# A two-layer transformer kernel: norms by half rows, and the first layer's stages in another order

## The reference, cut to what matters

```python
# layer one (first_block)
xn = rmsnorm(h, ln1_w); proj = xn @ w_in
dq, dk, dv, gq, gk, gv, gr, zf, zb = jnp.split(proj, splits, axis=-1)
log_g_f = jax.nn.log_sigmoid((zf @ gla_gate_w2_f + gla_gate_b_f)) / GLA_TAU      # and _b
da = rmsnorm(diff_attention(dq, dk, dv, lam, pos), da_subln_w) * (1.0 - lam_init)
go = rmsnorm(gla_bidirectional(gq, gk, gv, log_g_f, log_g_b), gla_norm_w) * jax.nn.silu(gr)
h = h + jnp.concatenate([da, go], axis=-1) @ w_out
hn = rmsnorm(h, ln2_w)
h = h + peer_ffn(hn, peer_w_q, peer_sub_keys, peer_u, peer_v)
# layer two (hybrid_layer), after the final norm of layer one
m = g[:, :, 0] * y_a + g[:, :, 1] * y_b + g[:, :, 2] * y_c
h = h + m @ w_o
hn = rms_norm(h, norm2_g)
gate, up = jnp.split(hn @ w_gate_up, 2, axis=-1)
h = h + (jax.nn.silu(gate) * up) @ w_down
out = rms_norm(h, final_g)
```

## Time and profile before

| | us |
|---|---|
| three runs | 2654.69, 2650.17, 2654.87 |
| median | 2654.69 |
| profiled execution, device time | 2648.79 |
| profiled execution, span | 2647.0 |
| TensorE busy | 2582.6 (98%) |
| VectorE busy | 1530.2 (58%) |
| GpSimd busy | 1026.9 (39%) |
| ScalarE busy | 925.0 (35%) |
| mean granted TensorE clock | 0.989 of full |

### The profile page before, as it was taken

One profiled execution on the slowest core, in us unless ns is written; L12 is line 12 of the kernel. 1 busy time (PEld: TensorE's weight loads), 2 busy tenths in 40 slices (PEclk: granted clock), 3 DMA queues, 4 the chain that ended last, 5 costly groups with the idle time before them and its releaser, 6 DMA issues.

```text
span 2647.0 us, 33693 instructions
## 1 busy us (share of the span) xinstructions
PE 2582.6 (98%) x12573; PEld 2118.5 (80%) x12573; DVE 1530.2 (58%) x3293; ACT 925.0 (35%) x1472; POOL 1026.9 (39%) x683
## 2 busy tenths in 40 slices
PE   8999889999999999999999999999999999999998
PEld 7776678888888888888888888877977788788886
DVE  3234736999688522225888888843974445433322
ACT  4223533333344322223333333453334442422222
POOL 4320110389888888604777777210350000000000
PEclk9998999999999999999999999999999999999999
DMA  4210046755657766658999999832332123333321
GB/s 155 72 32 33 33 126 211 241 127 137 148 124 195 195 144 145 147 164 288 376 370 366 373 370 370 308 105 80 86 90 56 41 83 132 87 97 96 96 96 72
DMA packets 330946, 427.87 MB, mean 162 GB/s; under 512 B 58720, under 2 KB 246912, under 8 KB 330272
## 3 DMA queue, kind: packets, MB, share of 16 engines
q1 hardware_dynamic: 271392, 358.39, 41.9%
q0 software_dynamic: 59392, 67.34, 10.4%
HBM read 362.59 MB, written 63.05 MB: 161 GB/s over the span
## 4 chain that ended last, share of the span: by engine, by line
PE 82%; ACT 1%; DVE 1%; issue 1%; DMA 0%; SPq 0%; DVEq 0%; ACTq 0%
PE bank L209 26%; PE bank L213 26%; PE bank L212 26%; PE bank L2500 1%; PE bank L1688 1%; PE bank L2475 1%; PE bank L1671 1%; PE bank L2458 0%; PE bank L2498 0%; ACT s_wh L2219 0%; ACT s_junk L375 0%; PE bank L2488 0%; PE bank L475 0%; PE bank L2510 0%; DVE s_h L2814 0%
## 5 line engine op out<-in xcount | busy, mean ns | idle before, releaser
L1727 DVE TENSOR_TENSOR pe_wl<-pe_raw,pe_wh 128x1024 fp32r<-128x1024 f32 x272 | 354.5, 1305 | 367.1 <-ACT pe_wh L1587 350.6
L1517 POOL DMA_INDIRECT scratch_sums<-pe_pick,pe_cell_u x256 | 430.0, 1680 | 78.0 <-issue 77.5
L209 PE MATMUL bank<-pe_xh,pe_wh 128*128 128x512 f32 x1152 | 453.2, 393 | 1.3 <-DVE pe_xl L452 1.3
L213 PE MATMUL bank<-pe_xh,pe_wl 128*128 128x512 f32 x1152 | 448.6, 389 | 0.0
L212 PE MATMUL bank<-pe_xl,pe_wh 128*128 128x512 f32 x1152 | 448.5, 389 | 0.0
L1587 ACT ACTIVATE pe_wh<-pe_raw 128x1024 fp32r<-128x1024 f32 x272 | 288.0, 1059 | 304.2 <-PE bank L213 272.9
L2562 DVE TENSOR_TENSOR s_wl<-s_raw,s_wh 128x1024 fp32r<-128x1024 f32 x143 | 179.4, 1256 | 273.6 <-ACT s_wh L2219 272.3
L209 PE MATMUL bank<-pe_wh,pe_hh 128*128 128x512 f32 x768 | 298.8, 389 | 0.0
L212 PE MATMUL bank<-pe_wl,pe_hh 128*128 128x512 f32 x768 | 298.8, 389 | 0.0
L213 PE MATMUL bank<-pe_wh,pe_hl 128*128 128x512 f32 x768 | 298.8, 389 | 0.0
L209 PEld LDWEIGHTS bank<-pe_xh,pe_wh 128*128 128x128 f32 x1152 | 216.4, 188 | 46.4 <-issue 1.2
(11 more groups left out here) (452 smaller groups left out, 4652.6 us busy)
## 6 DMA issues: line engine op xcount, KB each, us to landing
pe_raw<-in_peer_u SPq DMA_DIRECT2D x128, 512.0 KB
pe_raw<-in_peer_v SPq DMA_DIRECT2D x128, 512.0 KB
scratch_hidden<-pe_a_out SPq DMA_DIRECT2D x128, 256.0 KB
pe_a_in<-scratch_hidden SPq DMA_DIRECT2D x128, 192.0 KB
s_raw<-in_w_in SPq DMA_DIRECT2D x48, 512.0 KB, 3.8
s_raw<-in_w_gate_up SPq DMA_DIRECT2D x44, 512.0 KB, 4.0
scratch_sums<-pp_zeros SPq DMA_DIRECT2D x16, 1024.0 KB, 6.2
pe_added_gate<-scratch_sums SPq DMA_DIRECT2D x32, 512.0 KB
```

The lines of the kernel that those rows point to most:

```text
L209: first = pe.matmul(out, lhs[0], rhs[0], start=start, stop=False, skip_group_check=skip)
L213: return pe.matmul(out, lhs[1], rhs[0], start=False, stop=stop, skip_group_check=skip)
L1517: pool.indirect_dma_start(cells, bass.IndirectOffsetOnAxis(ap=cell_u[:, t, at:at + 1], axis=0), pick[:, t, 2, at:at + 1], None, compute_op ...
L1727: dve.tensor_tensor(wl[:, i % RING, :], raw[:, i % RAW, :], wh[:, i % RING, :].bitcast(F32), ALU.subtract).then_inc(S["w_lo"], 1)
```

## The change

It has parts in every stage but the experts' stream and the first half of layer two.

1. Gate logits: three banks by turns in place of two; three of them before gk, the fourth and fifth after gk's first and second slab.
2. The lambda is made before q is taken, its exponentials beside those of the decays, its last two steps after the keys are rotated.
3. The mask of the last chunk tile comes after `take(k_b)`.
4. ScalarE squares three of four tiles of linear attention's output in the projection's block, one head at a time, with the sum in the same instruction. Only the last tile is squared and summed in the attention's block, and the root stands before the loop.
5. The transposes of head 0 stand at the end of the projection's list, those of head 1 before the loop, of heads 2 and 3 in turns 0 and 1, each with banks of its own.
6. `phase_mix_out` waits for the turned columns one by one; it squares the rows of h by halves; it loads the first four weight tiles of the experts and splits two of them. `SummedStats` in the next block adds the halves and takes one root for all four tiles.
7. `wo` 0 to 3 has banks 4 to 7 and `wo` 4 to 7 has banks 0 to 3.
8. `HalfStats` for norm two and the last norm: squares of the first half rows during `wo` 5 and `down` 12, with a root on a dummy value behind them; adds of the next tile ahead of the wait for the root; the last norm's gain is multiplied into the first half at `down` 14, and at the end ScalarE scales the first half and VectorE the second.

```diff
+class HalfStats(RowStats):
+    def square(self, act, half, t):
+        done = half * NT + t
+        if done:
+            act.wait_ge(self.squared, done)
+        act.activation(self.junk[:, 0:BANK], self.rows[:, t, half * BANK:(half + 1) * BANK], ACT.Square,
+                       accum_out=self.ss[:, half, t:t + 1]).then_inc(self.squared, 1)
+    def first_squares(self, act, ready):
+        for t in range(NT):
+            ready(act, t)
+            self.square(act, 0, t)
+        act.wait_ge(self.squared, NT)
+        act.activation(self.root[:, NT:NT + 1], self.junk[:, 0:1], ACT.Sqrt)
+    def first_means(self, dve, chain):
+        dve.wait_ge(self.squared, NT)
+        chain(dve.tensor_scalar(self.ss[:, 0, :], self.ss[:, 0, :], 1.0 / self.width, EPS, ALU.mult, ALU.add))
+    def on_scalar(self, act, ready, after=None):
+        for t in range(NT):
+            ready(act, t)
+            self.square(act, 1, t)
+            act.wait_ge(self.meaned, t + 1)
+            act.activation(self.root[:, t:t + 1], self.ss[:, 1, t:t + 1], ACT.Sqrt).then_inc(self.rooted, 1)
+            if after and t:
+                after(t - 1)
+        if after:
+            after(NT - 1)
+    def on_vector(self, dve, chain, use, front):
+        front(0)
+        for t in range(NT):
+            dve.wait_ge(self.squared, NT + t + 1)
+            dve.scalar_tensor_tensor(self.ss[:, 1, t:t + 1], self.ss[:, 1, t:t + 1], 1.0 / self.width,
+                                     self.ss[:, 0, t:t + 1], ALU.mult, ALU.add).then_inc(self.meaned, 1)
+            if t + 1 < NT:
+                front(t + 1)
+            dve.wait_ge(self.rooted, t + 1)
+            chain(dve.reciprocal(self.rstd[:, t:t + 1], self.root[:, t:t + 1]))
+            use(t)
+class SummedStats(RowStats):
+    def on_scalar(self, act, ready):
+        act.wait_ge(self.meaned, 1)
+        act.activation(self.root[:, :], self.ss[:, :], ACT.Sqrt).then_inc(self.rooted, 1)
+    def on_vector(self, dve, chain, use, front=None):
+        chain(dve.tensor_tensor(self.ss[:, :], self.halves[:, 0, :], self.halves[:, 1, :], ALU.add))
+        dve.tensor_scalar(self.ss[:, :], self.ss[:, :], 1.0 / self.width, EPS, ALU.mult, ALU.add)\
+            .then_inc(self.meaned, 1)
+        dve.wait_ge(self.rooted, 1)
+        chain(dve.reciprocal(self.rstd[:, :], self.root[:, :]))
+        for t in range(NT):
+            use(t)
...
 phase_project_1, TensorE
-            for t, n in tiles:
-                if t >= 2:
-                    pe.wait_ge(S["y_taken"], t - 1)
+            def gate_logits(t):
+                n = tiles[t][1]
+                if t >= 3:
+                    pe.wait_ge(S["y_taken"], t - 2)
...
-            gemm.on_tensor(pe, gk_b)
+            for t in range(3):
+                gate_logits(t)
+            def logits_after(i):
+                if i < 2:
+                    gate_logits(3 + i)
+            gemm.on_tensor(pe, gk_b, between=logits_after)
...
+            pe.wait_ge(S["rotated"], 2)
+            pe.wait_ge(gemm.bank_free, gemm.freed(gr_b))
+            for b, src in ((0, L["q"]), (4, L["k"])):
+                for t in range(NT):
+                    pe.transpose(bank[:, b, t * P:(t + 1) * P], src[:, t, 0:P], ident)
 phase_project_1, VectorE
-            for t in range(NT):
+            for t in range(NT - 1):
+                mask_chunk(t)
             take(k_b)
+            chain(mask_chunk(NT - 1))
 phase_diff_attention, ScalarE
+            act.activation(qT[:, 0, :], bank[:, Q_BANK[0], :], ACT.Copy, scale=DA_DIM ** -0.5).then_inc(q_ready, 1)
+            act.activation(sq[:, :, :], mix_g[:, NT - 1, :].rearrange("p (h v) -> p h v", h=GLA_HEADS), ACT.Square)\
+                .then_inc(squared, 1)
+            take_query(1)
+            act.wait_ge(mean, 1)
+            act.activation(root[:, :], ss[:, :], ACT.Sqrt).then_inc(rooted, 1)
...
+                if r + 2 < DA_HEADS:
+                    take_query(r + 2)
 phase_diff_attention, TensorE
+            head_columns(1)
+            pe.wait_ge(q_ready, 2)
+            pe.wait_ge(k_ready, 2)
...
+                if r + 2 < DA_HEADS:
+                    pe.wait_ge(k_ready, 2 + r)
+                    head_columns(r + 2)
 phase_diff_attention, VectorE
+            take_key(0)
+            dve.wait_ge(k_turned, 1)
+            dve.tensor_copy(kT[:, :, 0:META], ...)
+            norm_sums()
+            take_key(1)
 phase_mix_out
             def turned(kt):
-                if kt < HALF_K:
-                    pe.wait_ge(turn.done, kt + 1)
+                pe.wait_ge(turn.done, kt + 1)
...
-                    pe.wait_ge(turn.done, KD)
+            for i in range(RAW):
+                sp.dma_start(raw[:, i, :].rearrange("p (k j) -> p k j", k=KD), query_slab(io, i))\
+                    .then_inc(weights_ahead[i], 16)
+            squares(0)
+            for i in range(SPLIT_AHEAD):
+                act.wait_ge(weights_ahead[i], 16)
+                act.activation(wh[:, i, :], raw[:, i, :], ACT.Copy).then_inc(split, 1)
+            squares(1)
 SecondPlan
-                first = 4 * (half if kind == "wo" else 1 - half)
+                first = 4 * (1 - half)
 phase_second
+                if (kind, n) == ("wo", 5):
+                    norm_2.stats.first_squares(act, ...)
+                if (kind, n) == ("down", KF // 2 + 1):
+                    last_stats.first_squares(act, ...)
+            def scale_first(t):
+                act.wait_ge(S["last_rstd"], t + 1)
+                act.activation(h[:, t, halves[0]], h[:, t, halves[0]], ACT.Copy, scale=last_stats.rstd[:, t:t + 1])\
+                    .then_inc(S["front_done"], 1)
+                if (kind, n) == ("down", KF // 2 + 3):
+                    last_stats.first_means(dve, chain)
+                    dve.wait_ge(S["row_landed"], 16)
+                    for t in range(NT):
+                        last = dve.tensor_tensor(h[:, t, halves[0]], h[:, t, halves[0]], final_row[:, halves[0]], ALU.mult)
+                    chain(last)
+            def scale_last(t):
+                dve.sem_inc(S["last_rstd"], 1)
+                dve.scalar_tensor_tensor(h[:, t, halves[1]], h[:, t, halves[1]], last_stats.rstd[:, t:t + 1],
+                                         final_row[:, halves[1]], ALU.mult, ALU.mult).then_inc(S["out_done"], 1)
```

189 lines of the change are left out of this document (122 added, 67 removed).

## The result

| | before | after |
|---|---|---|
| median of the runs, us | 2652.88 (2650.17 to 2654.87) | 2628.97 (2626.47 to 2629.51) |
| profiled execution, us | 2648.79 | 2628.91 |
| its span, us | 2647.0 | 2626.8 |
| TensorE busy, us | 2582.6 | 2575.2 |

The ratio is 0.9909, with a 95% interval of 0.9892 to 0.9926. The forecast was 22.0 us less than before, 2632.7 us. Between the two profiled executions it is 19.9 us less, between the medians 23.9. The sum is compared with the profiled executions, since its terms were read from one; the kernel before varies by 4.7 us in its four runs, so the median does not test it more closely.

A forecast was written before the change was run, and what follows sets the result against it. TensorE was taken to bound the kernel, busy 2582.6 of 2647.0 us, so only its waits and low-clock stretches counted. Terms at the boundaries summed to 22.0 us, from the median of 2654.7 to 2632.7 us; range 2618 to 2645.

The forecast's parts named there:

- Logits: Gate logits before gk: three banks remove 2.5 us of waits, plus part of the slow products; gain 3.0 us (1.0 to 3.7).
- Mask: Before v's first product: copies of k go ahead of the last chunk mask; gain 2.9 us (2.3 to 2.9).
- banks: Before wo's first product: other banks remove the wait for VectorE's multiplications; gain 1.7 us (1.5 to 1.7).
- norm two: Before layer two's silu products: the fourth add no longer waits behind a scaling and root; gain 2.4 us (1.8 to 2.9).
- end: After the last product: earlier add, half squares and scaling split over two engines; gain 4.0 us (3.0 to 4.8).
- Attention: Projection to attention: earlier first exponential, no stop for the root; gain 4.0 us (1.5 to 4.8), clock counted as 0.
- rival (b): Attention: the clock does not fall, or only briefly; up to 9.5 us more gained, so 2622 us; chance 0.12.
- Columns: Output projection's second turn: waiting for remainders singly removes 1.7 us, plus slow products; gain 2.5 us (1.7 to 3.3).
- Experts' start: Output projection to experts: squares under products, first transpose 1.0 us and first product 1.1 earlier; gain 1.5 us (0.3 to 3).
- Rival (a): Attention's low clock gets longer, or an order there costs what another gives; 2643 us; chance 0.17.
- (c): Clock stays low to the attention's end and through the output projection's products; 12 us slower, 2667 us; chance 0.03.
- (d): Block ends absorb the parts' gains; only banks, mask and end count, 8.6 us, so 2646 us; chance 0.08.

The follow-up runs named there:

- u_early: Kernel after with the gate logits, the column-by-column waits of the output projection and the half rows of norm two undone; 2633.99 us, ratio to before 0.9946.
- fill_end: fill_three plus 7 identity transposes at the attention loop's first turn without scores and 8 behind its last products; 2619.33 us, ratio to before 0.9883.
- fill_all: fill_three plus gv's second slab rounded earlier, 10 identity transposes among the chunk sums, 8 behind the attention's last products; 2624.40 us, ratio to before 0.9894.
- u_mid: Kernel after with the mask order, the turning of heads in the attention's loop, wo's banks and the last norm undone; 2639.05 us, ratio to before 0.9965.
- u_root: Kernel after with the linear heads' root taken inside the attention's loop instead of before it; 2628.16 us, one run.
- u_sums: Kernel after with the experts' norm squaring full rows at the start of its own block; 2628.50 us, one run.
- fill_x: Kernel after with 22 identity transposes in the idle time between the output projection's last product and the experts' first transpose; 2625.66 us, ratio to before 0.9909.
- fill_a: Kernel after with 6, 4, 4 and 4 identity transposes ahead of the scores of attention turns 1, 2, 7 and 9; 2627.09 us, ratio to before 0.9916.
- fill_three: Kernel after with the fillings of fill_s, fill_x and fill_a together; 2624.70 us, ratio to before 0.9898.
- fill_s: Kernel after with 14 multiplications of a tile of ones in the idle time before the first transposes; 2626.36 us, ratio to before 0.991.

## Why the prediction was right, step by step

The mechanism held in seven of eight places: the waits that the edits were to remove went, but for most of the one before the experts, and the span fell by 20.2 of 22.0 us. That the total is nearer than the steps is luck: an over-rated term, the logits, and chance in two stretches that nobody edited (1.95 us together) were made up by the attention and the columns.

- Logits, forecast 3.0 (1.0 to 3.7), measured 0.05: the step that failed. The term of 2.5 us for waits was read from the 6.87 us of the logits by taking all above 0.86 us for each as waiting. At full clock no more than 0.15 us of each is waiting; nearly all the rest is the low clock, which had come at 36.8, during the third logit (windows above). The low stretch is 6.8 us long in both profiles with two banks (before, u_early), 3.4 in eight of those with three, and absent in the other four, the kernel after among them. To gv's first product this is 19.8, 18.5 and 16.9 us, so the edit did win 1.3 to 2.9 us there, by the clock and not by waits. The sentence that the later fifth add "costs nothing" was wrong: I looked at the matmuls 40 us away and not at what stands behind the exponentials in ScalarE's list. That is the split of gv's second slab, and the wait for it costs 1.3 us from gv to the chunk sums (28.9 against 27.6 in u_early). In the kernel after the clock then stayed low longer, from 90.3 to 97.1 (3.4 us in the kernel before), which cost 0.47 and 1.06. In the fourteen profiles the stretch from the first logit to the turn of ks takes 80.9 to 81.2 us in twelve, 79.5 in fill_end, which had no fall at 37 and a short one at 90, and 79.7 in fill_all, which had no fall at 37 and not the new wait.
- Mask 2.96, banks 1.87, norm two 2.49, end 3.74: as forecast, and each comes back when undone, the mask and norm two with 1.5 and 1.0 us of low clock on top.
- Attention, forecast 4.0 and 0 for the clock, measured 6.61. The start behaved as worked out: the first exponential comes 4.62 us after the block's start (4.5 by the sum), and the difference of turn 1 is 4.5 us earlier than before, counted from the state of the meta tokens (4.2 to 4.7 by the lists). By the page "ScalarE: Activation LUTs" (What ACT_TABLE_LOAD costs) of the Trainium skill each switch would have held it 1.4 us longer; again the activation starts 1.30 us after the load does. The other 2.1 us were won in the turns behind it, where the clock counted for nothing in the forecast: it was low for 17 us in place of 34. That is part of rival (b), which had 0.12 (its price of 9.5 us makes 2623.2, not 2622). Of the start, u_mid shows 1.6 us for turning heads 2 and 3 in the loop and u_root 0.7 for the root. Repeats of the same attention differ by 3 us, so the 2.1 can be chance.
- Columns, forecast 2.5, measured 3.36: 1.7 of wait (u_early) and 1.6 of clock, which the kernel before lost and u_early, with the same wait, did not.
- Experts' start, forecast 1.5, measured 1.06, but otherwise than thought. The first transpose is 0.54 earlier, not 1.0: the half squares take 0.82 us each and lag 0.4 behind the last addition. The transposes, no longer paced by scalings, ran at the low clock, so of 1.1 us for the first product 0.17 was left (u_sums: the sums are worth 0.60, fill_x: the low clock takes 1.67). The missing gap of 0.30 became 0.96 over the first dozen product groups; what makes it so was not looked into.
- Rival (a) was wrong in its sign, (c) and (d) had nothing.

What the clock does is the part that stays open. It fell behind waits in the attention and before the experts, and filling these with transposes held it at those two places: before the experts it fell in none of the four kernels with the filling of fill_x and in all ten without, at 235 to 241 us in none of the four with the filling of fill_a and in all ten without. It also fell among the chunk sums with most of the wait filled, between 260 and 272 us in all four kernels with fill_a's filling, and in fill_three and fill_all at a wait that was left. The Trainium skill ("TensorE: Matmul & The Clock Gate", Part 4: PE-mode transpose) says that the full clock does not engage for transposes, which do not count as busy in the same way; fill_x, which has nothing but transposes from the last product to 368.2 and the clock at 1.00 throughout, is against it.

## What to carry to other kernels

When a step is moved later, follow every engine that waits for it through its whole list, to the next thing that TensorE needs, not only to the moved step's own user. A wait of one or two microseconds on TensorE can cost as much again in slow products behind it, and not in every run: read each part from its own stretch, in more than one profile, before crediting an edit with the clock. Where a wait can't be removed, a few useless transposes in it are a cheap try; it is best to fill all neighbouring waits, not the first alone, and to judge by the spread of the runs as well as by the median.

## What was not expected of the hardware

- The pace of TensorE after the idle start. The kernel after's first transposes of 128 columns start 0.21 us apart until 15.2 and 0.11 apart from then on (in the kernel before until 13.0), with a granted clock of 1.00 in the windows all along. These are the two spacings of the experts' transposes at a granted 0.50 and 1.00 (kernel after, 366.5 to 371.9), so the 1.00 of the first microseconds doesn't tell the pace. ("7 in a us" in what was expected of fill_s counts all that a window touches; 4 or 5 start in each.) With 14 matmuls in the idle time ahead all 32 took 3.71 us in fill_s, but 5.03, 5.38 and 6.63 in fill_three, fill_end and fill_all, where 0.50 is granted from 9.7, 11.4 and 9.5 us on. The filling ends 1.5 to 2.9 us before the transposes can start, so it leaves a wait of its own; whether a filling up to the transposes would hold was not tried. The 1.3 us or more that fill_s won are not a gain to count on.
- The course of the clock differs between executions of one instruction order. The profiles differ by up to 3 us in the attention alone (95.8 to 98.9 us), by 1.5 at the logits and by 1.2 at the start. The runs of one kernel spread by 1.9 to 12.4 us, and in the kernels with the widest spread the mean granted clock of a run goes with its time: u_mid's slowest run, 2649.9 us, has 0.985, its other nine, 2637.4 to 2642.9 us, 0.990 or 0.991; fill_all has 0.995 at 2618.4 and 2619.5 us, 0.992 at 2628.0.
